# A fifth gate and up pair in seven-product form, and 32 modulation tiles drawn together into 68 units

## The reference, cut to what matters

```python
mod = (c @ w_mod[l] + b_mod[l]).reshape(B, N_MOD, D)     # c: (1, 2048), w_mod: (2048, 6 * 2048)
shift_m, scale_m, gate_m = mod[:, 0, None], mod[:, 1, None], mod[:, 2, None]
shift_f, scale_f, gate_f = mod[:, 3, None], mod[:, 4, None], mod[:, 5, None]
...
h2 = rms_norm(x, g_pre_ffn[l]) * (1 + scale_f) + shift_f
f = (jax.nn.silu(h2 @ w_ffn_gate[l]) * (h2 @ w_ffn_up[l])) @ w_ffn_down[l]   # hidden width 5632
x = x + gate_f * rms_norm(f, g_post_ffn[l])
```

## Time and profile before

| | |
|---|---|
| median of the runs | 2318.03 us |
| profiled execution, its own time | 2317.87 us |
| span of its profile | 2316.1 us |
| granted TensorE clock | 0.999 |
| TensorE busy | 2299.1 us, 99% |
| VectorE, ScalarE, GpSimd busy | 79%, 51%, 19% |
| HBM traffic over the span | 234 GB/s |

### The profile page before, as it was taken

The page is one execution under the profiler, slowest core; times in us unless marked ns, Lnnn a source line. Parts: engine busy times, 40 slices in busy tenths (PEclk is TensorE's granted clock), DMA queues, the critical chain, the costliest instruction groups (busy, mean ns, idle before and its releaser), DMA issues.

```text
span 2316.1 us, 31102 instructions
## 1 busy us (share of the span) xinstructions
PE 2299.1 (99%) x10665; PEld 1886.4 (81%) x10665; DVE 1824.8 (79%) x2349; ACT 1185.2 (51%) x1510; POOL 449.1 (19%) x878
## 2 busy tenths in 40 slices
PE   9999999999999999999999999999999999999998
PEld 6878788888878888888888888888888888888887
DVE  5888899999777676888688886666788768888764
ACT  3544546544574444555455565445655544444653
POOL 0001001334001211212100001112012145686310
PEclk9999999999999999999999999999999999999999
DMA  9996569999958887666666656666556676666564
GB/s 392 396 335 245 162 232 370 355 338 342 360 179 287 309 281 253 217 209 213 207 224 204 235 187 232 220 220 205 190 199 228 216 218 189 193 203 200 183 211 153
DMA packets 178821, 566.95 MB, mean 245 GB/s; under 512 B 30816, under 2 KB 35200, under 8 KB 178304
## 3 DMA queue, kind: packets, MB, share of 16 engines
q1 hardware_dynamic: 145584, 528.28, 66.4%
q0 software_dynamic: 27136, 23.91, 3.5%
q10 hardware_dynamic: 5968, 13.00, 1.6%
HBM read 537.01 MB, written 4.21 MB: 234 GB/s over the span
## 4 chain that ended last, share of the span: by engine, by line
PE 90%; DVE 4%; DMA 3%; issue 1%; ACT 1%; ACTq 0%; SPq 0%; DVEq 0%
PE acc L2903 25%; PE acc L2904 25%; PE acc L2910 25%; DMA raw<-in_wa_dram 2%; DVE lo L1701 1%; PE tb L3398 1%; PE tb L3405 1%; PE tb L3399 1%; PE acc L3405 1%; PE acc L3398 1%; PE acc L3399 1%; DMA start_raw<-in_wa_dram 1%; PE tb L3597 1%; DVE macc L1934 1%; PE tb L2990 1%
## 5 line engine op out<-in xcount | busy, mean ns | idle before, releaser
L897 ACT ACTIVATE hi<-raw 128x1024 fp32r<-128x1024 f32 (+2 forms) x808 | 825.2, 1031 | 768.5 <-PE acc L2910 428.0
L1701 DVE TENSOR_TENSOR lo<-raw,hi 128x1024 fp32r<-128x1024 f32 (+1 forms) x748 | 892.0, 1209 | 318.8 <-ACT hi L897 312.9
L2903 PE MATMUL acc<-hi,Hh 128*128 128x512 f32 x1816 | 714.0, 393 | 1.9 <-issue 1.5
L2904 PE MATMUL acc<-hi,Hl 128*128 128x512 f32 x1816 | 707.4, 390 | 0.0
L2910 PE MATMUL acc<-lo,Hh 128*128 128x512 f32 x1816 | 485.7, 389 | 0.0
L2903 PEld LDWEIGHTS acc<-hi,Hh 128*128 128x128 f32 x1816 | 341.0, 188 | 80.3 <-issue 8.2
L2910 PEld LDWEIGHTS acc<-lo,Hh 128*128 128x128 f32 x1816 | 340.9, 188 | 71.3
L2904 PEld LDWEIGHTS acc<-hi,Hl 128*128 128x128 f32 x1816 | 341.1, 188 | 69.2 <-issue 0.2
L2903 PE MATMUL acc<-hi,hbh 128*128 128x512 f32 x512 | 202.8, 396 | 0.0
L2904 PE MATMUL acc<-hi,hbl 128*128 128x512 f32 x512 | 199.6, 390 | 0.0
L803 POOL DMA_DIRECT2D tok<-sgt x176 | 85.9, 497 | 493.0 <-DVE sgt L1877 381.8
(11 more groups left out here) (496 smaller groups left out, 2917.5 us busy)
## 6 DMA issues: line engine op xcount, KB each, us to landing
raw<-in_wa_dram SPq DMA_DIRECT2D x680, 512.0 KB, 4.5
raw<-in_wb_dram SPq DMA_DIRECT2D x96, 512.0 KB, 4.5
late_raw<-in_wa_dram SPq DMA_DIRECT2D x90, 512.0 KB, 6.6
start_raw<-in_wa_dram SPq DMA_DIRECT2D x70, 512.0 KB, 7.8
raw<-in_wc_dram SPq DMA_DIRECT2D x64, 512.0 KB, 4.2
tok<-sgt POOLq DMA_DIRECT2D x416, 32.0 KB, 4.3
landed<-sgt POOLq DMA_DIRECT2D x192, 32.0 KB, 4.1
pt_landed<-att_parts POOLq DMA_DIRECT2D x192, 12.0 KB, 3.1
```

The lines of the kernel that those rows point to most:

```text
L897: act.activation(hi[:, s, n], w, ACT.Copy).then_inc(hi_ready, 1)
L1701: dve.tensor_tensor(lo[:, s, 0:n], raw[:, r, 0:n], hi[:, s, 0:n].bitcast(F32), ALU.subtract)\
L2903: pe.matmul(dst(tt), a, hi[:, s, w], start=first[tt] and i == 0, stop=False, skip_group_check=shared)
L2904: pe.matmul(dst(tt), b, hi[:, s, w], start=False, stop=False, skip_group_check=shared)
```

## The change

`GATED` begins at 5, so that pair 5 (units 292 to 311 then) is a seven-product pair too. The units of all later work move by four, and a count of all units rises by four. The 32 late tiles of the FFN must be over earlier and are spread over 68 units instead of 84: 220, 222, 224, 226, 228, 230, 232, 234, 237, 239 and so on to 283 and 285, a step of two units 24 times and of three 7 times. The loads stay the same in number and size; the two of a group in pair 5 stand next to each other.

```diff
-A_UNITS = A_LOADS + 2 * (2 * 8 + 2 * 4 + 2 * 3)
+A_UNITS = A_LOADS + 2 * (2 * 8 + 2 * 5 + 2 * 3)
...
-GATED = range(6, 10)
+GATED = range(5, 10)
 GATED_SEVEN = {6: 3, 7: 8}
...
-LATE += spaced(GATES0 + 20, 44, 44) + spaced(MERGE0, 32, 25) + spaced(OUT0, 24, 21) + spaced(FFN0 + 8, 84, 32)
+LATE += spaced(GATES0 + 20, 44, 44) + spaced(MERGE0, 32, 25) + spaced(OUT0, 24, 21) + spaced(FFN0 + 8, 68, 32)
```

## The result

The changed kernel takes 2327.18 us (median of six, 2324.19 to 2329.64), the kernel before, run beside it, 2318.26 us (2317.78 to 2319.93). The ratio is 1.0036, with a 95% interval of 1.0026 to 1.0046: 8.9 us slower. The forecast was 2324.0 us, 6.0 us slower. The profiled execution is the slowest of the six, 2329.64 us, so its trace shows the loss at its largest.

A forecast was written before the change was run, and what follows sets the result against it. TensorE was taken to bound the kernel, with the late tiles' load circle running at its own pace. 2317.87 - 1.36 (pair 5) + 7.5 (waiting) = 2324.0 us; range 2316.5 to 2327.6 us.

The forecast's parts named there:

- Direction and mechanism: Units 222 to 285: the ring's circle of loads falls behind, TensorE waits, the kernel is 0.26% slower; slower given 0.61.
- Pair 5, 1.36 us won, fed at no cost: Pair 5 loses six matmuls of 0.227 us, 1.36 us won; extra VectorE and ScalarE work costed at nothing.
- Rival 3: First group of pair 5 waits for `hi` and `lo`: up to 1.4 us more; chance counted within the stall's 0.61.
- The pace carried over: Units 222 to 285: 93 loads at the measured 1.957 us take 182.0 us, where TensorE needs 172.2 us.
- the corrections: Units 222 to 285: late tiles skip ScalarE, 1.1 us less; fewer pair ends with other VectorE work, 1.1 us less.
- the 7.5 us of waiting: TensorE's wait between units 222 and 285: 9.7 us late, less two corrections of 1.1 us each.
- a lead of nothing: At unit 222 `hi` ends just before TensorE starts; the stall was counted from this lead of 0.1 us.
- Rival 1, the ring gives way: Late-tile stretch: landings shorten as bunches even out, wait only 1 to 6 us; at 3 us, 2319.5 us; chance 0.20.
- Rival 2, no stall: Late-tile stretch: pace under 1.85 us a load, only the six matmuls' gain is left, 2316.5 us; chance 0.17.

The follow-up runs named there:

- dense tiles alone: The kernel before with its 32 late tiles in 68 units and only pairs 6 to 9 in seven-product form: 2324.74 us, ratio 1.0027.
- own slots: The changed kernel with late tiles landing in two slots of their own, the halves of `macc`, the ring's four slots left for units: 2317.04 us, ratio 0.9993.
- 76 and 60 units: The kernel before, four gated pairs, with the 32 late tiles in 76 units: 2321.11 us; in 60 units: 2329.98 us.
- the five pairs with that spacing: The changed kernel with late tiles at the earlier spacing up to unit 293, the last three at plain units of pair 5: 2317.82 us, ratio 0.9997.
- the short operation of VectorE: The changed kernel with VectorE multiplying and adding only 128 of 1024 columns of each late FFN tile, after full loads: 2324.07 us, ratio 1.0021.
- the kernel with six pairs and own slots: The changed kernel with pairs 4 to 9 in seven-product form and late tiles in two slots of their own: 2315.66 us, ratio 0.9987.

## Why the prediction was right, step by step

**Direction and mechanism: right.** TensorE waits, in 16 pieces, between units 222 and 285; the circle of slot, load, `hi`, `lo` sets the pace. The dense tiles alone bring the loss, own slots take it away.

**Pair 5, 1.36 us won, fed at no cost: right.** 42.16 against 43.52 us. Rival 3 didn't happen.

**The pace carried over: right in the main, and a little quicker when dense.** 1.957 us a load times 93 was 182.0 us. I took 2.2 us off, for the tiles that skip ScalarE and for fewer pair ends, which gives 1.933 us a load. The first profile of the changed kernel has 1.960, as if nothing had to come off, but the second has 1.907, and the dense tiles in 68, 76 and 60 units 1.915, 1.917 and 1.903. At the spacing of before, units 222 to 285 with their 24 tiles are 87 loads, and took 169.6 us in the profile before and 170.0 us in that of the five pairs with that spacing: 1.949 and 1.954. So the sign of the corrections is borne out by four profiles of five, and their sum lies between the two profiles of the changed kernel. Each of the two by itself is not shown; both rest on rounds of slots that add up, which the short operation of VectorE leaves open.

**A term mis-sized, within the range: the 7.5 us of waiting.** TensorE's lateness was 11.4 us in the slowest execution and 6.5 us in the fastest (2317.87 - 1.36 + 6.5 = 2323.0, plus 0.5 us that it was late at unit 222 already; 2324.02 was measured). The forecast of 2324.0 us is the time of the fastest of 12 executions; in the first median some 3 us more were lost. Two things were missing in it. TensorE doesn't end the stretch with a lead of nothing: it waits for the latest moments of a bunched stream, and at unit 285 `hi` was ready 870.50 - 869.09 = 1.4 us early, so the lateness is 1.3 us more than circle minus need. And the pace is not one number: I took that of one execution.

**Rival 1, the ring gives way: at most in a small part.** The median landing, 690 to 870 us, stayed at 5.0 us in both profiles of the changed kernel; it was 4.8 us for the dense tiles alone and in 76 units, and 4.9 us in 60 units. The circle did get up to 3% quicker, and TensorE waited all the same.

**Rival 2, no stall: didn't happen.** By the fit that the Trainium skill states (DMA: Bandwidth & Descriptors, Anatomy of one DMA, for the GpSimd path), 512 KB take an estimated 3.2 us. The quickest landing was 3.3 us here, the median 5.0, and the measurement decides. Up to four loads are under way here, and where the bytes of some were halved, the full ones came in 4.6 us, so loads under way together slow each other.

**The range**, 2316.5 to 2327.6, holds the median of 2327.18 near its upper end, and doesn't hold the two slowest executions.

## What to carry to other kernels

A ring that feeds the bound engine has a pace of its own. Slots over the round of a slot give only its upper limit: here that sum allowed 162.7 us for the 93 loads, and the changed kernel took 177.3 and 182.3 us. So measure the pace where the engine behind it never holds it up, in us for each load, and compare it with what a denser schedule asks, also when the bound engine is busy for 99% and the DMA engines are not full. A ring that just keeps up on average already cost 2.4 us here, because loads come in bunches. A stream put through the ring of another is cheaper in slots of its own; here memory that a finished stage leaves was enough for them.

## What the runs showed that I had not expected

The changed kernel varies more from execution to execution: 2324.0 to 2329.6 us in 12 runs, where the kernel before took 2317.7 to 2320.0 us in the 28 runs beside the second six of them, and the kernel with six pairs and own slots 2314.8 to 2316.5 us in 11. It would be tempting to say that a ring that is the bound passes its scatter on. But the dense tiles alone, bound by the same ring, took 2324.4 to 2325.8 us in nine runs, as narrow as any, while 60 units have 2326.3 to 2331.4 in five. What makes the changed kernel scatter is open.

After a wait TensorE starts slowly: at unit 249 the second matmul comes 0.34 us after the first (765.12 - 764.78) rather than 0.23, so such a wait costs a little over its own length.
